# A decoder step with a mixture of experts: other places for the gather buffers, later and smaller weight requests, and 64 idle matrix products around the routing

## The reference, cut to what matters

```
def hier_moe(x, rg_w, rg_b, re_w, re_b, e_wg, e_wu, e_wd):
    pg = jax.nn.softmax((xt @ rg_w + rg_b).astype(f32), axis=-1)
    g_sel = jnp.argmax(pg, axis=-1)
    ...
    le = (jnp.einsum('nd,gde->nge', xt, re_w) + re_b).astype(f32)
    le_sel = jnp.einsum('nge,ng->ne', le, oh_g)
    pe = jax.nn.softmax(le_sel, axis=-1)
    top_v, top_i = lax.top_k(pe, EXP_TOPK)
    ...
    for gi in range(N_GROUPS):
        h = jax.nn.silu(jnp.einsum('nd,edf->nef', xt, e_wg[gi])) * jnp.einsum('nd,edf->nef', xt, e_wu[gi])
        out = out + jnp.einsum('nef,efd->nd', h * comb[:, gi, :, None], e_wd[gi])
```

## Time and profile before

| | |
|---|---|
| time, median of 3 runs | 1491.37 us (1490.8 to 1492.15) |
| the profiled execution's own time | 1493.73 us |
| its span, first to last instruction | 1491.9 us |
| PE busy, share of the span | 84% |
| DVE, ACT, POOL busy | 28%, 22%, 6% |
| mean granted clock of PE | 0.908 |
| DMA, mean over the span | 190 GB/s |
| in the slices of the expert stage | 411 to 413 GB/s |

### The profile page before, as it was taken

How to read it: one execution, slowest core, us unless ns; L and a number is a source line. 1 busy time by engine, 2 the same in 40 slices (tenths; PEclk the granted TensorE clock), 3 DMA queues, 4 the chain that set the end, 5 groups by cost and what they waited for, 6 DMA issues and landing times.

```text
span 1491.9 us, 24663 instructions
## 1 busy us (share of the span) xinstructions
PE 1248.5 (84%) x10998; PEld 950.9 (64%) x10998; DVE 418.3 (28%) x723; ACT 326.4 (22%) x563; POOL 96.8 (6%) x141
## 2 busy tenths in 40 slices
PE   4999998999799557799999999487887878787780
PEld 4899998889798445799999998232332332232230
DVE  5248322333342231233333333310110110010015
ACT  5453322323212221222222222210000000000001
POOL 2000000000000000000000000221111111111110
PEclk9999999998879678599999999599999999999995
DMA  6111023002213413133322374699999999999975
GB/s 207 58 29 28 6 47 101 4 5 65 78 61 85 132 31 111 29 85 86 85 81 75 101 276 169 245 338 395 412 413 412 411 413 413 412 412 411 409 290 195
DMA packets 136661, 284.02 MB, mean 190 GB/s; under 512 B 24931, under 2 KB 84533, under 8 KB 127786
## 3 DMA queue, kind: packets, MB, share of 16 engines
q1 hardware_dynamic: 130458, 270.60, 49.6%
q0 software_dynamic: 5440, 9.46, 1.7%
q10 hardware_dynamic: 656, 2.36, 0.4%
HBM read 274.11 MB, written 15.61 MB: 194 GB/s over the span
## 4 chain that ended last, share of the span: by engine, by line
PE 62%; DMA 19%; DVE 7%; SPq 5%; issue 3%; ACT 2%; POOL 1%; POOLq 0%; DVEq 0%; ACTq 0%
DMA slot<-in_e_wu_dram 12%; PE bank L1206 6%; PE bank L1208 6%; PE bank L1207 6%; DMA xg<-normed_tokens,il 6%; SPq L549 4%; PE bank L592 4%; PE bank L599 4%; PE bank L1230 3%; PE bank L1232 3%; PE bank L1231 3%; PE bank L1778 2%; PE bank L1338 2%; PE bank L1340 2%; PE bank L1339 2%
## 5 line engine op out<-in xcount | busy, mean ns | idle before, releaser
L592 PE MATMUL bank<-slot,xs 128*64 128x512 f32 x512 | 248.9, 636 | 57.3 <-DMA slot<-in_e_wu_dram 56.3
L593 PE MATMUL bank<-slot,xs 128*64 128x512 f32 x512 | 250.0, 638 | 0.0
L592 PEld LDWEIGHTS bank<-slot,xs 128*64 128x64 f32 x512 | 70.1, 145 | 201.2 <-issue 199.2
L1206 PE MATMUL bank<-xnh,wh 128*128 128x256 f32 (+1 forms) x448 | 133.6, 298 | 10.8 <-issue 10.2
L1207 PE MATMUL bank<-xnl,wh 128*128 128x256 f32 (+1 forms) x448 | 133.3, 297 | 0.0
L1208 PE MATMUL bank<-xnh,low 128*128 128x256 f32 (+1 forms) x448 | 133.3, 297 | 0.0
L599 PE MATMUL bank<-slot,ht 128*64 128x512 f32 x512 | 122.0, 620 | 0.5 <-DVE ht L905 0.5
L2155 DVE TENSOR_TENSOR low<-ring,wh 128x1536 fp32r<-128x1536 f32 (+1 forms) x45 | 90.1, 2006 | 109.8 <-ACT wh L1834 100.6
L895 DVE TENSOR_TENSOR h<-sg,bank 64x512 f32<-64x512 f32 x32 | 21.8, 680 | 321.4 <-ACT sg L789 314.2
L789 ACT ACTIVATE sg<-bank 64x512 f32<-64x512 f32 x32 | 19.0, 594 | 419.0 <-PE bank L593 419.0
L1206 PEld LDWEIGHTS bank<-xnh,wh 128*128 128x128 f32 x448 | 85.8, 192 | 11.0 <-issue 10.3
(11 more groups left out here) (472 smaller groups left out, 2540.4 us busy)
## 6 DMA issues: line engine op xcount, KB each, us to landing
slot<-in_e_wg_dram SPq DMA_DIRECT2D x64, 1024.0 KB, 20.9
slot<-in_e_wu_dram SPq DMA_DIRECT2D x64, 1024.0 KB, 21.9
slot<-in_e_wd_dram SPq DMA_DIRECT2D x64, 1024.0 KB, 19.5
ring<-in_w_in_dram SPq DMA_DIRECT2D x13, 1024.0 KB, 9.0
ring<-in_w_in_dram SPq DMA_DIRECT2D x24, 512.0 KB, 4.4
ring<-in_w_branch_dram SPq DMA_DIRECT2D x24, 256.0 KB, 4.8
kvs<-in_cache_mem_k_dram SPq DMA_DIRECT2D x8, 512.0 KB, 4.5
kvs<-in_cache_mem_v_dram SPq DMA_DIRECT2D x8, 512.0 KB, 3.7
```

The source lines that it names most:

```text
L592: pe.matmul(out[64:128, :], tok, wg[:, FF * k:FF * k + FF], start=(k == 0), stop=(k == KD - 1))
L593: mm = pe.matmul(out[0:64, :], tok, wu[:, FF * k:FF * k + FF], start=(k == 0), stop=(k == KD - 1))
L1206: pe.matmul(part, w_h, xh_(k, cols), start=(k == 0), stop=False)
```

## The change

- The gather buffers xg get a place of their own, beside the routing's tiles. POOL clears them as soon as that place is free (the second after the last unit, the first after ACT's last square), and the wait for `x2_stored` now stands before the first gather.
- (2, 1) is requested only after `x2_stored`, and (2, 2) only after the gathers of experts 0 and 1 have landed.
- gate_up counts a new step "gh" after its first half, and SP requests the first halves of (e, 0) and (e, 1) at gh(e - 3), the second at gate_up(e - 3).
- ACT takes a root of ones ahead of the squares of the first of the four last units, so that its table of functions with the root is loaded there.
- DVE clears `lg8` and `sel` while it waits for PE in the last unit, and makes the two integer-to-float copies behind `scaled`.
- PE does 64 products of `ones` and `before` (128 x 128 x 128, float32) into a bank that nobody reads: 30 ahead of "sel", 6 ahead of "rows", 28 ahead of the first `turn_in`.

```diff
--- before.py
+++ after.py
@@ -366,9 +366,9 @@
         place1 = route_tile("place1", [128, 2 * 5, CAP])
         row1 = route_tile("row1", [128, 2 * 5, 2, EX])
         empty = route_tile("empty", [128, 2 * EX])
-        assert cu <= z + 18432
-
-        xg = [sb(f"xg{n}", [128, 512], F32, z3 + 36864 + 2048 * n) for n in range(2)]
+        assert cu <= z + 16384
+
+        xg = [sb(f"xg{n}", [128, 512], F32, at) for n, at in enumerate((z + 23040, z + 16384))]
         xs = [sb(f"xs{n}", [128, 4, 128], F32, z3 + 40960 + 2048 * n) for n in range(2)]
         sg = sb("sg", [CAP, FF], F32, z3 + 45056)
         h2 = sb("h2", [CAP, FF], F32, z3 + 47104)
@@ -527,10 +527,10 @@
                       + [("ht", OUTS - 1), ("x2", OUTS - 1)])
         pe_t = Steps(sem("pe_t"), ["pos", "lists"])
         act_t = Steps(sem("act_t"), ["root"] + [("x2", t) for t in range(5)] + ["exp_g", "exp_e"])
-        dve_t = Steps(sem("dve_t"), ["sumsq", "ms", "rstd", "lg", "dg", "sel", "places", "rows", "lists", "addr", "de", "c12", "tab"])
+        dve_t = Steps(sem("dve_t"), ["clear", "sumsq", "ms", "rstd", "lg", "dg", "sel", "places", "rows", "lists", "addr", "de", "c12", "tab"])
         pool_t = Steps(sem("pool_t"), ["far", "rows", "xg"])
         pe_m = Steps(sem("pe_m"), [x for e in range(EX + 1) for x in
-                                   ([("t", 0)] if e == 0 else []) + ([("gu", e)] if e < EX else []) + ([("t", e + 1)] if e + 1 < EX else [])
+                                   ([("t", 0)] if e == 0 else []) + ([("gh", e), ("gu", e)] if e < EX else []) + ([("t", e + 1)] if e + 1 < EX else [])
                                    + ([("d", e - 1)] if e else []) + ([("ht", e)] if e < EX else [])])
         act_e = Steps(sem("act_e"), [x for e in range(EX) for x in ([("xs", 0)] if e == 0 else []) + [("silu", e)]
                                      + ([("xs", e + 1)] if e + 1 < EX else [])])
@@ -559,12 +559,15 @@
             load(1, 2)
             load(2, 0)
             dve_t.wait(sp, "lg")
+            sp.wait_ge(x2_stored, 80)
             load(2, 1)
             dve_t.wait(sp, "c12")
+            for n in range(2):
+                sp.wait_ge(gathered[n], 16)
             load(2, 2)
             for e in range(3, EX):
-                pe_m.wait(sp, ("gu", e - 3))
                 for f in range(2):
+                    pe_m.wait(sp, ("gu" if f else "gh", e - 3))
                     load(e, 0, (f,))
                     load(e, 1, (f,))
                 pe_m.wait(sp, ("d", e - 3))
@@ -638,6 +641,7 @@
                 turned(c - 1)
             else:
                 dve_o.wait(act, "wr")
+                act.activation(rstd[:, 7:8], ones[:, 0:1], ACT.Sqrt)
             for t, (_, tn) in enumerate(TILES):
                 if t == 4:
                     if c == OUTS - 1:
@@ -687,6 +691,8 @@
             hv = h[0:NS, 4, 256 * c:256 * c + 256]
             dve_evac.done(dve.tensor_tensor(hv, hv, banks[2][0:NS, 0:256], ALU.add), u)
             if c == OUTS - 1:
+                dve.memset(lg8[:, :, :], -1e30)
+                dve_t.done(dve.memset(sel[:, :, :], 0.0), "clear")
                 turned(c)
                 act_o.wait(dve, ("sq", c, 4))
                 dve_o.wait(dve, "wr")
@@ -694,12 +700,20 @@
                 dve_t.wait(dve, "sumsq")
                 dve_t.done(dve.tensor_scalar(ssq[:, 0:5], ssq[:, 0:5], 1.0 / D, RMS_EPS, ALU.mult, ALU.add), "ms")
                 scaled(c)
+                pool_t.wait(dve, "rows")
+                dve.tensor_copy(iota_f[:, :], iota_i[:, :])
+                dve.tensor_copy(row_f[:, :, :, :], row_i[:, :, :, :])
 
         def moe_pe(pe):
 
             turn_h_rows(pe, OUTS - 1)
             logits(pe, OUTS - 1)
 
+            def idle_products(n):
+                for _ in range(n):
+                    pe.matmul(psum[7][:, 0:128], ones[:, :], before[:, :], start=True, stop=True)
+
+            idle_products(30)
             dve_t.wait(pe, "sel")
             places = psum[5][:, 0:6 * EX].rearrange("p (t e) -> p t e", e=EX)
             pe.matmul(places, before[:, :], sel[:, :, :], start=True, stop=False, skip_group_check=True)
@@ -707,12 +721,14 @@
                 mm = pe.matmul(places[:, o + 1:6, :], ones[:, :], sel[:, o, :].unsqueeze(1).to_broadcast([128, 5 - o, EX]),
                                start=False, stop=(o == 4), skip_group_check=True)
             pe_t.done(mm, "pos")
+            idle_products(6)
             dve_t.wait(pe, "rows")
             for n in range(10):
                 tn = TILES[n % 5][1]
                 for p in (0, 64):
                     mm = pe.matmul(psum[6][p:p + 64, 0:2 * EX], place1[0:tn, n, :], row1[0:tn, n, :, :], start=(n == 0), stop=(n == 9))
             pe_t.done(mm, "lists")
+            idle_products(28)
 
             def turn_in(e):
                 pe.wait_ge(gathered[e % 2], 16 * (e // 2 + 1))
@@ -728,7 +744,7 @@
                     for n in range(2):
                         pe.wait_ge(eslot_loaded[(3 * e + n) % NSLOT][f], 16 * ((3 * e + n) // NSLOT + 1))
                     mm = expert_in(pe, psum[e % 2], xs[e % 2], slots[3 * e % NSLOT], slots[(3 * e + 1) % NSLOT], range(4 * f, 4 * f + 4))
-                pe_m.done(mm, ("gu", e))
+                    pe_m.done(mm, ("gu" if f else "gh", e))
 
             def down(e):
                 dve_e.wait(pe, ("ht", e))
@@ -801,11 +817,6 @@
             act_f.done(act.activation(rstd[:, 0:5], ssq[:, 0:5], ACT.Sqrt), "root")
 
         def moe_dve(dve, seq):
-            pool_t.wait(dve, "rows")
-            seq(dve.memset(lg8[:, :, :], -1e30))
-            seq(dve.memset(sel[:, :, :], 0.0))
-            dve.tensor_copy(iota_f[:, :], iota_i[:, :])
-            dve.tensor_copy(row_f[:, :, :, :], row_i[:, :, :, :])
             act_t.wait(dve, "root")
             dve_t.done(dve.reciprocal(rstd[:, 0:5], rstd[:, 0:5]), "rstd")
             dve_t.wait(dve, "rstd")
@@ -939,10 +950,11 @@
                 for k in range(2):
                     last = pool.iota(row_i[:, n, k, :], [[256 * (n + 1), 5]], base=2 + 2 * n * k, channel_multiplier=2 * (n + 1))
             pool_t.done(last, "rows")
+            pool.memset(xg[1][:, :], 0.0)
+            act_o.wait(pool, ("sq", OUTS - 1, 4))
+            pool_t.done(pool.memset(xg[0][:, :], 0.0), "xg")
+            pool_t.wait(pool, "xg")
             pool.wait_ge(x2_stored, 80)
-            seq(pool.memset(xg[0][:, :], 0.0))
-            pool_t.done(pool.memset(xg[1][:, :], 0.0), "xg")
-            pool_t.wait(pool, "xg")
             dve_t.wait(pool, "lists")
 
             def table():
```

## The result

| | before | after |
|---|---|---|
| median of 5 runs, us | 1491.37 (1490.16 to 1492.24) | 1481.07 (1478.27 to 1484.45) |
| profiled execution, its span, its clock | 1493.73, 1491.9, 0.908 | 1481.07, 1479.2, 0.924 |
| start of DVE's last sum of the last output unit, us | 925.95 | 920.53 |
| from there to the gather's start | 26.40 | 21.17 |
| to the end of gate_up(0) | 44.38 | 38.06 |

The ratio is 0.9932, with an interval of 0.9916 to 0.9948: faster by 10.3 us, where 8.2 were forecast. The third line warns how to read it. Of the 12.7 us between the two spans, 5.4 lie ahead of the last output unit, where the change adds one small root and nothing else. So from here on times are given after that line ("after the unit").

A forecast was written before the change was run, and what follows sets the result against it. The weight stream sets the pace, so its start, held by down(0) and the routing chain, was taken to bound. Gather start 4.6, flight 0.7, turns 0.4 and gate_up(0) 2.5 us made 8.2: 1483.2 us from 1491.37, range 1481 to 1486.

The forecast's parts named there:

- The sum: Start of the routed experts: gather's start 4.6 us, flight 0.7, turns 0.4, gate_up(0) 2.5, together 8.2 us sooner.
- Places and lists: Routing steps on PE before the gather: fuller clock from the products saves 1.2 us on places, 0.7 on lists.
- The stores: Stores of x2, freed from (2, 1): done 5.5 us sooner, at 944.8 us, 2 us before the lists.
- The flight: First gather's transfer beside (2, 1), which has three microseconds of a start: 6.0 us instead of 6.69, 0.7 less.
- gate_up(0): First expert's gate_up on PE: with the clock still up, 7.1 us instead of 9.6, 2.5 less.
- Rival (a): PE's clock falls again before gate_up(0), by chance in each execution: up to 2.9 us lost, 1486.1 us; chance 0.17.
- Half slots: First halves of expert 3 requested 3.4 us before the second: worth nothing, since SP still stands before down(0).
- One for one: From routing to the kernel's end: each delay passes on in full; the end moves as down(0) and down(1) do.
- (b): Weight stream after down(0): later downs hold on to their gathers' flights, half the gain becomes gaps: 1487.3 us; chance 0.09.
- (c): First gather and routing: a flight of 3.5 us and both PE steps at their upper bounds: 1479.6 us; chance 0.09.
- (d): Products run at half clock and delay "sel" and the turns; decided from 0.30 us a product: 1496.9 us; chance 0.05.
- (e): Kernel's tail: nothing moves, the tail decides by its own clock; chance 0.04, shared with small gains by other means.

The follow-up runs named there:

- old_requests: Changed kernel with (2, 1) and (2, 2) requested as before, without the waits for stores and gathers: 1488.66 us, ratio 0.9979.
- requests_only: Kernel before plus only the held requests: (2, 1) waits for the stores of x2, (2, 2) for the first two gathers: 1486.08 us, ratio 0.9958.
- no_products: Changed kernel without its 64 idle products on PE: 1482.34 us, ratio 0.9940.
- after_again: Changed kernel run once more, unchanged, with a second trace: 1482.10 us, ratio 0.9947 against the kernel before.
- gathers_first: Changed kernel with (2, 1) requested only when gather 0 has landed and (2, 2) when gather 1 has: 1482.78 us, ratio 0.9933.
- both_orders: Changed kernel with need_order and gathers_first together, and 21 products instead of 28 ahead of the first turn: 1478.50 us, ratio 0.9917.
- products_doubled: Changed kernel with 60, 12 and 56 idle products instead of 30, 6 and 28: 1491.98 us, ratio 1.0012.
- whole_slots: Changed kernel with both halves of a pair of slots requested together, when gate_up(e - 3) is done: 1485.42 us, ratio 0.9972.
- need_order: Changed kernel with each third matrix requested behind the first two of the next expert, in PE's order of need: 1475.71 us, ratio 0.9877.
- small_moves_undone: Changed kernel without the early root and with DVE's memsets and casts back in their old place: 1483.55 us, one run.

## Why the prediction was right, and where its steps were not

*The sum.* The time fell into the range, near its lower end, and the stage behind the unit gave 7.3 us in the first pair of profiles and 7.7 by the means of both pairs, against 8.2. That the sum comes so near is partly luck, since its terms missed both ways. The gather starts 5.2 us sooner (forecast 4.6), the flight gives 0 (0.7), the turns 0.4 (0.4), gate_up(0) 0.7 (2.5): 6.3 at down(0). One more microsecond came behind down(0), from steps that the forecast held at 0. And with the loads asked for as before, the other parts of the change gave 0.8 us together (old_requests), while the held requests alone gave 6.1 of the 6.3 us at down(0) (requests_only): the split of the sum into clock, buffers and stores was not the real one.

*Places and lists.* 1.4 and 1.2 us against 1.2 and 0.7: the clock was full, as forecast. But they were counted as gains on the path, and no_products shows that they are worth nothing. The path ran from the stores to the request for (2, 1), through that load, and then to the gather's packets. That the stores also land 0.5 us later with the products than without (20.2 and 20.3 us against 19.6 and 19.7) is seen in these traces and not explained.

*The stores.* That they come sooner without (2, 1) was right, and it is most of the change. They came 20.2 us after the unit, where 18.85 was forecast (944.8 - 925.95), 4.2 sooner than before (950.36 - 925.95 = 24.4) instead of 5.5. `il` was complete at 20.2 us too: the 2 us by which the stores were to be ahead of the lists did not exist. In after the lists came last by a hair, in after_again the stores did, and neither cost anything.

*The flight.* Forecast 6.0 us, since (2, 1) was to have a start of 3 us. It had 0.9, and the flight stayed at 6.69. That a load with more of a start makes the flight shorter was right: with starts of 4.1 and 4.5 us, flights were 3.70 and 3.46. But the two do not share the engines for most of that time; the gather stands until most of the load has moved. Alone, a flight is 3.2 us (gathers_first, and 3.18 in both_orders). The forecast also took a gather for 0.26 MB: of its 128 rows only those of tokens that chose the expert move, and the packets of the first two gathers hold 0.30 MB together, 0.15 each. By the Trainium skill (DMA: Bandwidth & Descriptors, Queues, rings and completion order), sharing packet by packet gave the estimate of 4.5 us for a flight beside a load; the runs, with 6.69 and 7.07, don't agree, and with 0.15 MB the estimate would be lower still.

*gate_up(0).* This is the mis-sized term: 8.7 us instead of 7.1. Rival (a) happened: PE's clock was half from 949.8 to 953.2 us, after 2 us of idle time ahead of the turns. The forecast called that chance in each execution. It is not: the fall comes 29.2 to 29.5 us after the unit in all seven traces with the products and a gather that lands beside a load. In gathers_first, both_orders and products_doubled, where the turns follow the products at once, it does not come, and gate_up(0) takes 7.1 us. What differs is the idle time ahead of the turns; the same four turns without it did no harm. By the Trainium skill (TensorE: Matmul & The Clock Gate, Part 4), turns don't bring the full clock; no run here shows turns by themselves, so whether they add to the idle time stays open.

*Half slots.* Forecast 0, "the engines idle there for some 5 us". They are worth 1.3 us (whole_slots). The step that failed is the rate: reloads of expert 3 were to run at 412 GB/s and be through at 971.3 us (45.4 after the unit), with time to spare. They landed at 973.0 us (52.5), behind down(0). The window from 950 to 970 us gives 296 GB/s with the engines 96% busy, and the idle stretch before (3, 2) is short (215 GB/s over 5 us). The stores of the token lists fall into that window, but hardly as bytes or as time. The queues from 950 to 970 us in the changed kernel:

```profile
q1 hardware_dynamic: 1229, 5.76, 92.8%
q0 software_dynamic: 400, 0.15, 3.0%
```

and SP's queue from 1100 to 1400 us:

```profile
q1 hardware_dynamic: 25681, 117.60, 97.0%
```

All of POOL's transfers, a gather among them, take 3% of the engines' time. It is the packets of the weights that take longer: 0.31 MB for a microsecond of busy engines, against 0.40 later. That the small stores cause this is a guess from the overlap; it was not tried by itself.

*One for one.* "I take the end of the kernel to move by as much as down(0) and down(1) move" held for products_doubled (9.0 and 9.4) and failed for gathers_first (3.8 and 1.1), whole_slots (0.0 and 1.3) and need_order (0.0 and 6.3). The end moves with the bytes that have been asked for, and with the order of the last ones.

*The rivals.* (b) did not come: 406 to 412 GB/s from 975 us on. (c)'s short flight exists, but only where a load is held back or has mostly moved. (d)'s point of decision, 0.30 us a product, was just missed: the 30 products ahead of "sel" took 0.29 us each, and PE was free 0.55 us ahead of "sel". (e): from the last weights to the end it is 43.2 us before and 43.3 after.

*A slip.* 28 products with the first 4.7 us at half clock end at 946.2 + 4.7 + 17.3 x 0.23 = 954.9 us, not at 955.2; nothing hangs on it.

*What stays open.* The first comparison gives 10.3 us, the second 9.2, and the stage 7.7. The first interval (0.9916 to 0.9948, or 7.8 to 12.5 us) ends just above 7.7, the second (0.9927 to 0.9967, or 4.9 to 10.9 us) holds it, and the front's clock scatters by as much as the difference. Whether the early root gives the front something was not tied down; small_moves_undone, without it, had its unit at 922.89, amid the others.

## What to carry to other kernels

Look at what flies ahead of and beside a transfer on the critical path before making the work around it faster: holding back two loads that nobody needed yet was worth 6 us at down(0), and 64 products for the clock nothing. When a stream sets the pace, ask for its pieces in the order of need up to the last one, since the end is set by the work behind the last piece; that was another 6 us. And compare stages from a common event, as the front of this kernel moves by up to 9 us between executions of nearly the same instructions.

## What the runs showed of the hardware that was not expected

A gather of 0.15 MB landed 3.2 us after its start with the engines to itself, its first packet after 2.0 us. Started 0.9 us behind the request for a load of 2.1 MB it landed after 6.69 us, its first packet after 4.8 us, when 1.7 of the 2.1 MB had moved; started 4.1 and 4.5 us behind it, after 3.70 and 3.46 us. While the token lists' small stores run, the engines are 96% busy and move 296 GB/s, where they move 412 in the long stretch. And the same 9124 matmuls of the front took from 919.7 to 928.5 us, with 147 to 150 us at half clock in the shortest and 167 in the longest.
